# The delta rule in chunks of 64 tokens, two heads across the partitions, in place of chunks of 106 tokens with four heads in turn

## What is computed

```python
g = jnp.cumsum(g, axis=-1)                               # log decay, within a chunk
decay = exp(where(tri, g[:, None] - g[None, :], -inf))
lmat = where(strict, beta[:, None] * (k @ k.T) * decay, 0)
sol = triangular_solve(lmat + eye, [v * beta, k * (beta * exp(g))])   # u, w
qk = (q @ k.T) * decay
def step(S, ...):                                        # once per chunk, in order
    v_new = u - w @ S
    o = (q * exp(g)) @ S + qk @ v_new
    S = S * exp(g_last) + (k * exp(g_last - g)).T @ v_new
```

## Time and profile before

| | us |
|---|---|
| median of 3 runs | 2903.34 (2903.24 to 2909.98) |
| profiled execution: own time / span | 2911.96 / 2910.1 |
| delta stage in it: from the first decay product to the last addition of outputs | 255.5 to 617.0 |
| PE / PE weight load / DVE / ACT / POOL busy, whole span | 2717.8 / 2342.6 / 1397.0 / 1023.8 / 1106.1 |
| granted PE clock, mean | 0.966 |

### The profile page before, as it was taken

The page is one execution under the profiler, slowest core; times in us unless marked ns, Lnnn a source line. Parts: engine busy times, 40 slices in busy tenths (PEclk is TensorE's granted clock), DMA queues, the critical chain, the costliest instruction groups (busy, mean ns, idle before and its releaser), DMA issues.

```text
span 2910.1 us, 48627 instructions
## 1 busy us (share of the span) xinstructions
PE 2717.8 (93%) x17831; PEld 2342.6 (80%) x17831; DVE 1397.0 (48%) x2063; ACT 1023.8 (35%) x1762; POOL 1106.1 (38%) x584
## 2 busy tenths in 40 slices
PE   6986888889999999999889899999999999999998
PEld 6964887868987778888778669999998976777876
DVE  2664566633311754233678656355367224555433
ACT  4772222223244242222423573222233246522222
POOL 3422433314444444444446214444444311344443
PEclk8997998999999999999999999999999989999999
DMA  2210000012223232332311002222322210222322
GB/s 96 93 51 6 12 10 10 11 48 88 93 87 93 94 92 91 98 96 92 97 51 53 22 2 80 91 90 87 90 85 79 66 37 2 66 89 92 95 93 94
DMA packets 88860, 197.92 MB, mean 68 GB/s; under 512 B 38140, under 2 KB 40238, under 8 KB 88728
## 3 DMA queue, kind: packets, MB, share of 16 engines
q1 hardware_dynamic: 84964, 192.72, 21.6%
q10 hardware_dynamic: 3764, 3.38, 0.4%
HBM read 192.24 MB, written 3.82 MB: 67 GB/s over the span
## 4 chain that ended last, share of the span: by engine, by line
issue 53%; POOL 13%; PE 5%; DVE 3%; POOLq 3%; DVEq 1%; ACT 0%; ACTq 0%
POOL wl L481 12%; PE ps L517 3%; POOLq L2166 2%; DVE work L2069 1%; DVE top L2066 1%; PE ps L1822 1%; POOL xbl L2175 1%; POOLq L130 0%; POOLq L2174 0%; PE ps L892 0%; PE ps L880 0%; POOLq L2163 0%; PE ps L2193 0%; DVEq L618 0%; DVEq L2067 0%
## 5 line engine op out<-in xcount | busy, mean ns | idle before, releaser
L481 POOL TENSOR_TENSOR wl<-wraw,wh 128x1024 fp32r<-128x1024 f32 x353 | 876.2, 2482 | 1206.4 <-ACT wh L473 1206.3
L473 ACT ACTIVATE wh<-wraw 128x1024 fp32r<-128x1024 f32 x353 | 372.5, 1055 | 578.3 <-PE ps L517 490.1
L517 PE MATMUL ps<-xah,wh 128*128 128x264 f32 (+1 forms) x2672 | 500.4, 328 | 24.0 <-ACT xah L846 14.2
L517 PE MATMUL ps<-xah,wl 128*128 128x264 f32 (+1 forms) x2672 | 488.1, 323 | 0.0
L517 PE MATMUL ps<-xal,wh 128*128 128x264 f32 (+1 forms) x2672 | 487.0, 322 | 0.0
L517 PEld LDWEIGHTS ps<-xah,wh 128*128 128x128 f32 x2672 | 405.5, 189 | 78.2 <-issue 23.6
L517 PEld LDWEIGHTS ps<-xah,wl 128*128 128x128 f32 x2672 | 403.8, 189 | 41.2 <-issue 0.6
L517 PEld LDWEIGHTS ps<-xal,wh 128*128 128x128 f32 x2672 | 402.7, 188 | 40.7
L665 DVE TENSOR_TENSOR res<-res,stage 128x512 f32 (+3 forms) x112 | 81.8, 731 | 442.1 <-ACT stage L581 442.1
L517 PE MATMUL ps<-xbh,wh 128*128 128x264 f32 (+1 forms) x1392 | 273.9, 337 | 13.6 <-POOL wl L481 13.0
L517 PE MATMUL ps<-xbl,wh 128*128 128x264 f32 (+1 forms) x1392 | 269.6, 333 | 0.0
(11 more groups left out here) (337 smaller groups left out, 3151.0 us busy)
## 6 DMA issues: line engine op xcount, KB each, us to landing
wraw<-in_w SPq DMA_DIRECT2D x353, 512.0 KB, 3.5
res<-in_x SPq DMA_DIRECT2D x4, 528.0 KB, 5.8
res<-in_x ACTq DMA_DIRECT2D x1, 2048.0 KB, 7.8
out<-res SPq DMA_DIRECT2D x1, 2048.0 KB, 6.9
block_in<-mt SPq DMA_DIRECT2D x120, 4.0 KB
xq<-block_out SPq DMA_DIRECT2D x120, 8.0 KB
block_out<-yy SPq DMA_DIRECT2D x20, 56.0 KB
cossin<-in_cossin ACTq DMA_DIRECT2D x1, 528.0 KB
```

What stands on the lines that cost most here:

```text
L473: act.activation(wh[:, s * DM:(s + 1) * DM], wraw[:, s * DM:(s + 1) * DM], ACT.Copy).then_inc(hi_done, 1)
L481: pool.tensor_tensor(wl[:, s * DM:(s + 1) * DM], wraw[:, s * DM:(s + 1) * DM], wh[:, s * DM:(s + 1) * DM].bitcast(F32), ALU.subtract).then ...
L517: mm = pe.matmul(ps[:, 2 * s + h, 0:width], ws[:, s * DM + kk * P:s * DM + (kk + 1) * P], x[:, at:at + width], start=(h not in [o[0] for o ...
```

## The change

A chunk has `CD = 64` tokens, so there are `ND = 9` chunks (576 tokens, the last 48 padded). A step takes all eight heads of one chunk: heads 2r and 2r+1 lie on partitions 0 to 63 and 64 to 127, four such pairs side by side. So `STEPS = 9`, and the state of a direction is eight heads wide. A 64-row block has four 16x16 blocks and two levels of doubling (`LEVELS = 2`); the blocks of a direction are 8 block rows on the partitions, so 8 DMAs where there were 7.

PE: every product of two 64-row operands takes one quarter of the array. `quarters` issues them in two rounds, in which direction 0 on one half of the rows alternates with direction 1 on the other half, with one semaphore post for each direction at the end. `kk`, `qk` and `k_state` write alternately to the lower and upper 64 partitions. `outputs` adds two kinds of products of different height into one bank, in three parts. `state_step` is made for one head of each pair, and again for the other (`turn` 0 and 1), in the same bank, and `state_next` likewise; turn 1 on PE waits for `state_next` of turn 0, and `state_next` of turn 1 stands on DVE between `block_right(8)` and `block_left(8)`.

POOL: `decay_rows` has its own tile `grow` (it was the first 16 rows of `mt`), so it stands before `clear_inverse` and no longer last in the iteration; the third `masked` is gone.

Preparation: `qkv` is laid out chunk by chunk, so the norms of q and k work in two pieces of 5 and 4 chunks (320 and 256 columns) where they had one of 2 x 264, and `pe_prep` makes its per-token factors with 9 x 4 small products and 9 transpositions where there were 10 transpositions. `exp_diff` and `new_values` are the same with other widths. Masks and constants have other shapes. Two semaphores for constants become one.

```diff
--- before.py
+++ after.py
-TS = NCH * C
 ROWS = [min(C, T - t * C) for t in range(NCH)]
 ENDS = [min(C * (t + 1), T) for t in range(NCH)]
-H1, NG, GH = 8, 2, 4
+CD = 64
+ND = -(-T // CD)
+TD = ND * CD
+GH = 4
 FF1 = 2816
 FF1_PARTS = [8, 8, 6]
 FF2_PARTS = [8, 8, 8, 8]
 PARTS = 80
-LEVELS = 3
+LEVELS = 2
 BASE = 16
-NBLK = 7
-LANES = 4 * NBLK
+NBLK = CD // BASE
+LANES = 2 * GH * NBLK
...
-            for h in range(2):
-                mm = pe.matmul(ps[:, 4 + 2 * (m % 2) + h, 0:HT], lhs, hinv[:, h * HT:(h + 1) * HT],
-                               start=True, stop=True)
+            for h, (lo, hi) in enumerate(halves_of(chunked)):
+                mm = pe.matmul(ps[:, 4 + 2 * (m % 2) + h, 0:hi - lo], ident[:, m:m + 1].broadcast_to([P, P]),
+                               dinv[:, lo:hi], start=True, stop=True)
...
+            for h, (a, b) in enumerate(CUTS):
+                x = chunks_of(m, a, b)
+                last = dve.scalar_tensor_tensor(x, x, gain, by_chunk(ps[:, 4 + 2 * u + h, 0:CD * (b - a)]),
+                                                ALU.mult, ALU.mult)
+            last.then_inc(happ, 1)
...
+        for c in range(ND):
+            cut = slice(c * CD, (c + 1) * CD)
+            pe.transpose(ps[0:CD, 4, c * 16:(c + 1) * 16], gdec[:, cut], ident[0:16, 0:16])
+            for hh, half in halves():
+                for b, rows in ((5, gdec), (6, beta)):
+                    mm = pe.matmul(ps[half, b, 2 * GH * c:2 * GH * (c + 1)], rows[:, cut], ident[0:16, hh:16:2],
+                                   start=True, stop=True)
...
+        cells = scr_in[u].rearrange("(m q) (a b) -> q a m b", q=2 * NBLK, b=BASE)
         q.wait_ge(d_mt[u], n + 1)
-        for bl in range(NBLK):
-            src, k = diagonal(delta[u]["mt"][n % 2], bl)
-            q.dma_start(cells[bl, 0:k, :, 0:k], src).then_inc(d_cut[u], 16)
+        for bl in range(2 * NBLK):
+            q.dma_start(cells[bl], diagonal(delta[u]["mt"][n % 2], bl)).then_inc(d_cut[u], 16)
...
-                for bl in range(NBLK):
-                    dst, k = diagonal(delta[u]["xq"][n % 2], bl)
-                    sp.dma_start(dst, back[u][bl, 0:k, :, 0:k]).then_inc(d_x0[u], 16)
+                for bl in range(2 * NBLK):
+                    sp.dma_start(diagonal(delta[u]["xq"][n % 2], bl), back[u][bl]).then_inc(d_x0[u], 16)
...
+        ROUNDS = (((0, 0), (1, 1)), ((0, 1), (1, 0)))
+
+        def half_of_rows(hh):
+            return slice(64 * hh, 64 * hh + 64)
+
+        def quarters(b, lhs, rhs, width, done):
+
+
+            last = [None, None]
+            for pairs in ROUNDS:
+                for r in range(GH):
+                    for u, hh in pairs:
+                        half = half_of_rows(hh)
+                        last[u] = pe.matmul(ps[half, 4 * u + b, r * width:(r + 1) * width], lhs(u, half, r),
+                                            rhs(u, half, r), start=True, stop=True)
+            for u in range(2):
+                last[u].then_inc(done[u], 1)
+
...
+        def kk(n):
+            for u in range(2):
+                wait(pe, d_vt[u], n)
+                for r, sl in enumerate(unit_slices(CD)):
+                    for hh in range(2):
+                        k = column(n, u, 1, 2 * r + hh)
+                        mm = pe.matmul(ps[half_of_rows(hh), 4 * u + 1, sl], k, k, start=True, stop=True)
+                mm.then_inc(d_kk[u], 1)
...
+        def k_state(n):
             if fresh_state(n):
                 return
-            wait(pe, d_st[u], updates(n))
-            s = delta[u]["state"]
-            products4(bank4(u, 3), lambda r, sl: column(n, u, 1, r), lambda r, sl: s[:, sl], P
-                      ).then_inc(d_ks[u], 1)
...
+            for u in range(2):
+                wait(pe, d_st[u], 2 * updates(n))
+                for r, sl in enumerate(unit_slices(P)):
+                    for hh in range(2):
+                        mm = pe.matmul(ps[half_of_rows(hh), 4 * u + 3, sl], column(n, u, 1, 2 * r + hh),
+                                       state_of(u, hh, r), start=True, stop=True)
+                mm.then_inc(d_ks[u], 1)
...
+        def level_product(n, lv):
+            for u in range(2):
+                if lv == 0:
+                    wait(pe, d_qkd[u], n + 1)
+                    wait(pe, d_x0[u], 32 * NBLK * (n + 1))
+                else:
+                    wait(pe, d_x[u], (L - 1) * n + lv)
+                wait(pe, d_ob[u], L * n + lv + 1)
+            quarters(0, lambda u, half, r: delta[u]["ob"][half, r * CD:(r + 1) * CD],
+                     lambda u, half, r: inverse(n, u)[half, r * CD:(r + 1) * CD], CD, d_pp)
+
+        def level_update(n, lv):
+            for u in range(2):
+                wait(pe, d_ppc[u], L * n + lv + 1)
+                if lv > 0:
+                    wait(pe, d_xt[u], L * n + lv)
+                elif n + 1 < STEPS:
+                    wait(pe, d_mt[u], n + 2)
+            xt = lambda u, half, r: inverse_t(n, u)[half, r * CD:(r + 1) * CD]
+            pp = lambda u, half, r: delta[u]["pp"][half, r * CD:(r + 1) * CD]
+            if lv < L - 1:
+                quarters(1, xt, pp, CD, d_xu)
+            if lv == 0 and n + 1 < STEPS:
+                for u in range(2):
+                    wait(pe, d_eg[u], n + 2)
+            quarters(2, pp, xt, CD, d_xtu)
...
+            quarters(3, lambda u, half, r: inverse_t(n, u)[half, r * CD:(r + 1) * CD],
+                     lambda u, half, r: rhs(u)[half, r * P:(r + 1) * P], P, d_xr)
...
+            def new_part(turn):
+                last = [None, None]
+                for r in range(GH):
+                    for u, hh in ROUNDS[turn]:
+                        d, half = delta[u], half_of_rows(hh)
+                        alone = fresh_state(n)
+                        last[u] = pe.matmul(place_of(u, hh, r)[0], d["vn"][half, r * P:(r + 1) * P],
+                                            d["qkm"][n % 2][half, r * CD:(r + 1) * CD],
+                                            start=alone or (turn == 0 and r == 0),
+                                            stop=alone or (turn == 1 and r == GH - 1))
+                return last
+
+            for u in range(2):
+                wait(pe, d_qkm[u], n + 1)
+                wait(pe, d_vn[u], n + 1)
+                if not last_chunk(n):
+                    wait(pe, d_vk[u], updates(n) + 1)
+            for mm in new_part(0):
+                mm.then_inc(d_half, 1)
+            if not fresh_state(n):
+                for u in range(2):
+                    wait(pe, d_qd[u], n + 1)
+                    for r in range(GH):
+                        for hh in range(2):
+                            o, cols = place_of(u, hh, r)
+                            pe.matmul(o, state_of(u, hh, r), delta[u]["qd"][n % 3][:, cols], start=False,
+                                      stop=False)
+            pe.wait_ge(d_half, 2 * (n + 1))
+            last = new_part(1)
+            for u in range(2):
+                last[u].then_inc(d_o[u], 1)
+
+        def state_step(n, turn):
             if last_chunk(n):
                 return
-            d = delta[u]
-            kt, vk = d["kt"][n % 2], d["rr"]
-            wait(pe, d_oa[u], n + 1)
-            products4(bank4(u, 3, P), lambda r, sl: kt[:, sl], lambda r, sl: vk[:, sl], P).then_inc(d_ds[u], 1)
             for u in range(2):
-                body(n, u, *more)
+                if turn == 0:
+                    wait(pe, d_oa[u], n + 1)
+                else:
+                    wait(pe, d_st[u], 2 * updates(n) + 1)
+            last = [None, None]
+            for r, sl in enumerate(unit_slices(P)):
+                for u, hh in ROUNDS[turn]:
+                    d, half = delta[u], half_of_rows(hh)
+                    last[u] = pe.matmul(ps[:, 4 * u + 3, sl], d["kt"][n % 2][half, sl], d["rr"][half, sl], start=True,
+                                        stop=True)
+            for u in range(2):
+                last[u].then_inc(d_ds[u], 1)
...
+                if outer:
+                    state_step(t - 2, lv)
...
+            if t + 1 < STEPS:
+                each(decay_rows, t + 1)
...
-                each(masked, t - 1, 2)
-            if t + 1 < STEPS:
-                each(decay_rows, t + 1)
...
+            for hh, half in halves():
+                own = ps[half, 4 * u + 2, :].rearrange("p (r q i) -> p r q i", q=2, i=CD)[:, :, hh, :]
+                last = dve.tensor_tensor(units(d["dec"][n % 2][half, :], CD), own,
+                                         tok_cum[half, u, cc, :].unsqueeze(2).broadcast_to([64, GH, CD]), ALU.min)
+            last.then_inc(d_darg[u], 1)
...
-        def state_next(n, u):
+        def state_next(n, u, turn):
             if last_chunk(n):
                 return
-            d, cc, h = delta[u], chunk(n, u), head0(n)
-            wait(dve, d_ds[u], updates(n) + 1)
+            d, cc = delta[u], chunk(n, u)
+            hh = turn if u == 0 else 1 - turn
```

(17 more changed lines are left out.)

522 lines of the change are left out of this document (238 added, 284 removed).

## The result

The changed kernel takes 2916.34 us (median of 5 runs, 2908.93 to 2921.16), the kernel before 2905.91 us (5 runs, 2903.24 to 2909.98) beside it. The ratio is 1.0032, 95% interval [1.0018, 1.0046]: slower by about 0.3%, where 2878 was forecast and 2858 to 2908 was the range. The profiled execution of the changed kernel took 2912.22 us, with a span of 2910.3 us; that of before 2911.96 us and 2910.1 us. So the two profiled executions are equal, and the forecast of -25.5 us for them is off by 25.7.

A forecast was written before the change was run, and what follows sets the result against it. Bound: the delta stage's 35.1 us step, SP's 28 DMA issues plus DVE's 16.6 us. Stage -42, tail +6, preparation +6, norms +4.5 make -25.5: 2886.5 profiled, less 8.6 for the median, 2878 us; range 2858 to 2908.

The forecast's parts named there:

- the stage: Delta stage, first cut to last placement: 283.3 us where the kernel before takes 325.2, a change of -42 us.
- the tail: Last placement to last addition of the delta stage: 36.5 us where it was 30.5, +6 us.
- the preparation and norms: Ahead of the delta stage: +6 us for small float32 products, +4.5 us for the norms of q and k.
- DVE's part of the loop: DVE's work per step, inversion 7.93, `state_next` 4.1, level update 0.6: 12.65 us against 16.6.
- Quarters overlap: PE products on different quarters of the array overlap: 35 ns a record taken, 57 without overlap.
- The second branch: Chain from inversion through `k_state`, `rest` and `solve` to `mt`: +9.3 us after the inversion, SP ready at +9.1.
- a tie: `mt` and SP's queue ready almost together, 0.2 us late; 0.6 added to a 33.0 us step, giving 33.6.
- the rival of +1.5 us a step: SP's 32 issues in a row cost 1.5 us more a step, 2890; 0.20 together with the branch and POOL rivals.
- What lies beside it: Step work outside the loop (outputs, level 0, state steps, POOL) has slack of 2 to 4 us each.
- The first loop, the second and the last: Delta stage's loops other than the six full steps: 26.9, 28.9 and 25.9 us (the last up to the placement).
- No overlap: Rival: PE's quarter products don't overlap, about 38 us a step, 2916 us; chance 0.14.
- The rivals for SP and for the low clock: SP issues +1.5 us a step, 2890; low-clock `k_state` makes `mt` late, 35.5 us steps, 2892; 0.20 with POOL's rival.

The follow-up runs named there:

- e1: Changed kernel with extra unread PE products: 16 after the level-1 update, 8 after the second state step, 3 ahead of the outputs; 2900.1 us.
- e8: Changed kernel with only the 3 extra unread PE products ahead of the outputs; 2890.6 us.
- e6: Changed kernel with 3, 10 and 8 extra PE products at three places and the cuts of direction 1 issued by ACT; 2875.0 us.
- e9: Changed kernel with only the 3 extra PE products ahead of the outputs and the cuts of direction 1 issued by ACT; 2877.6 us.
- e2: Changed kernel with 16 extra PE products after the level-1 update and 8 after the second state step, none ahead of the outputs; 2913.8 us.
- e12: Kernel before with its seven cuts of direction 1 issued by ACT and nothing else; 2880.0 us.
- e3: Kernel before with 20 extra unread products in PE's 5 us wait ahead of level 1; 2889.3 us.

## Why the prediction was wrong

The median is 38.3 us above the forecast. Of these 25.7 are the profiled execution. The other 12.7 are no mechanism: I took 8.6 us off because the median of before lay that much under its profiled execution, and the median of the changed kernel lies 4.1 above its own. That difference was the spread of single executions, and the forecast carried it along as a term.

By its own steps, against the profiled execution: 25.7 us too few are 22.0 in the stage, 6.0 in the tail, -1.2 in the preparation and norms, and -1.2 in the stages behind.

- **DVE's part of the loop: right.** 12.65 us were forecast; from load to the end of `yy`'s copy it is 12.5 (413.47 to 426.02). The first copy takes 0.36 us, POOL is out of the way.
- **Quarters overlap: right.** 32 records in 1.15 us are (1.15 - 0.25)/31 = 29 ns, where I took 35 and had 57 for no overlap. 64-row records of 128 columns have 55 ns, (1.96 - 0.25)/31; 56 were forecast. By the rows below a change between array modes costs 0.12 us: 32 such records from 468.94 should be through their starts by 1.77 us, and the next kind starts at 470.83, after 1.89.

```profile
468.94 1.96 PE L1221 MATMUL ps<-rr,xq 64*64 64x128 f32 x32
470.83 1.15 PE L1261 MATMUL ps<-qkv 128*64 128x64 f32 x32
```

  The rule of the Trainium skill ("TensorEngine Tiling (Array Packing)", Key Properties) that a change of mode drains TensorE may hold here, but as a drain of that length; it decided nothing.
- **The second branch: right in kind, wrong in size.** It is not late in any full step. The 0.6 us that I added for a tie were not needed.
- **SP's queue: the rival of +1.5 us a step, about half true.** The cuts cost what I took, 7.80 us for 16 on the mean of the six full steps. The placing DMAs cost 8.70, 0.54 us each, where before took 0.44. I had used one mean of 0.49 for both kinds, right for the sum of 28 and 0.8 us short for 32. They move 8 KB each in both kernels. The layout by itself is not the reason: in the first loop of the changed kernel 16 placings in the same layout took 7.40 us, 0.46 each, which is also the mean of the full steps before. In the full steps most issues take as long as before, and some far longer (median 0.43 us, longest 2.04); in the step above the 16 took 10.51 us. Why stays open. The landing behind the cuts grew as well: see the next point.
- **"What lies beside it": the step that failed.** I gave `outputs` and level 0 a slack of 2 to 4 us and tested it only against a slower record (46 ns), not against the lower clock level, which I counted for `k_state` and half of `turn_kv` alone. In the trace the low level starts at the outputs in three of six steps, some 2 us behind a wait of 0.88 us, and doubles all records up to the end of level 0. Outputs and level 0 then end at about 451 in the step shown, where the blocks could have been taken up at 448.9 (446.18, the end of the cuts, + 2.7). Over the six full steps DVE takes up the blocks 5.4 us after the last cut, where 2.64 was summed: +2.8 a step. Three of them have the low outputs, 7.1 us on the mean; in the other three it is 3.7, and there DVE waits for the blocks themselves. So the low clock is 1.7 of the 2.8, 10 us in the six steps, and a later landing of the blocks 1.0, in which PE has no part. e1 and e8, which hold the clock at the outputs, shorten the stage by 11.2 and 8.6 us.
- **The stage.** From cut to cut a full step is 36.4 us, (548.06 - 329.86)/6. Against 33.6 that is +2.8 for the late start of the inversion, +0.9 for SP (with the short gap between placing and cuts), -0.6 for the tie and -0.3 for DVE in the first of them: +2.8, six times 16.6. The first loop, the second and the last add 2.4, 1.0 and 1.9: 21.9.
- **The tail: +12.0 instead of +6.** The outputs of L1343 take 7.09 us in it once, at the low level, where 3.79 is their time at the upper one, and the products around them likewise; e8, which keeps the level up there, has 34.5, near the 36.5 of the forecast.
- **Preparation and norms: right.** +9.3 to the first cut where 10.5 were summed; the norms' products take 19.98 us for 18.02.

Of the rivals none was the answer. "No overlap" named the right total, 2916, for a wrong reason: its records are refuted by every row of quarters above. The rivals for SP and for the low clock named the right causes with too small sizes, and put the clock on the second branch, where it cost nothing. Had I counted the low clock at the outputs too, by what the trace shows (10 us in the stage and some 7 in the tail), the forecast would have been near 2895, still 21 us below the median. With the low clock at the outputs and SP's queue both put right (e6, e9) the changed kernel needs 2875 to 2878 us. That is another kernel than the one that was forecast, though, and the one before gains as much from the same edits.

## What to carry to other kernels

When a change cuts an engine's work and leaves the loop around it, it makes waits; on TensorE count every record behind a new wait at both clock levels before calling it slack, and do so for the tail too. Where a loop is one queue's issues, first move some of them to another queue: here seven DMA issues a step moved to ACT made the kernel before 0.9% faster, where the whole re-tiling made it 0.3% slower. And compare a forecast with the kind of number that it was worked out from: the gap between one profiled execution and a median is spread, not a term. Judge a re-tiling with the cheap fixes in both versions, or it is credited or blamed for what it did not do.

## What the hardware showed that I had not expected

- The clock fell 2.0 to 2.6 us into the work behind a wait of only 0.88 us in three of six steps (435.88 and 438.5 in the one shown), and three extra products in that wait, six records in 0.94 us, kept it at the upper level until 450. Before, I had seen it fall only behind waits of several microseconds. The wait by itself does not bring it down: in the other three steps the same 0.88 us had no such effect. What of the time ahead of it counts as well was not separated.
- Having the clock at 0.87 instead of 0.76 over the stage was worth 3 us in the medians (e2), and 0.84 was worth 26 (e8); by the last addition of the profiled executions 0.7 and 15.4. Which stretch is low matters, not how much.
- Float32 products on different quarters of the array start every 29 ns with 64 columns, about a quarter of what a full-width record of 128 columns takes.
- A placing DMA of 8 KB held SP's queue for 0.44 us before and 0.54 in the full steps of the changed kernel, but 0.46 in its first loop; cuts of 4 KB held ACT's for 0.46 and 0.59 us each in the rows shown (3.65/8 in e6, 4.11/7 in e12).
- What POOL runs beside DVE shifted with the length of the step: in the kernel before, two edits that touched neither engine took 1.5 (e12) and 2.6 us (e3) out of DVE's part of a step, of which up to 1.5 was its wait for PE.
